# Weight rounding moved ahead of the squares in the paired feed-forward tiles of a two-layer trunk

## The reference, cut to what matters

```python
def squared_relu_mlp(u, w1, w2):
    a = jax.nn.relu(u @ w1)
    return (a * a) @ w2

u = rms_norm(h, ffn_norm_g[i])
h = h + squared_relu_mlp(u, ffn_w1[i], ffn_w2[i])   # w1: 1024 x 4096, w2: 4096 x 1024
```

## Time and profile before

| what | value |
|---|---|
| median of 3 runs | 1159.05 us (1157.74 to 1159.46) |
| profiled execution, its own time | 1157.56 us |
| its span, first to last instruction | 1155.8 us |
| mean granted TensorE clock | 0.994 of full speed |
| TensorE matmul / weight load busy | 1128.4 us / 1050.6 us |
| VectorE busy | 757.6 us (66%) |
| ScalarE busy | 526.5 us (46%) |
| weight loads | 16 DMA engines, 27.2% of their time |

### The profile page before, as it was taken

The page is one execution under the profiler, slowest core; times in us unless marked ns, Lnnn a source line. Parts: engine busy times, 40 slices in busy tenths (PEclk is TensorE's granted clock), DMA queues, the critical chain, the costliest instruction groups (busy, mean ns, idle before and its releaser), DMA issues.

```text
span 1155.8 us, 18677 instructions
## 1 busy us (share of the span) xinstructions
PE 1128.4 (98%) x7817; PEld 1050.6 (91%) x7817; DVE 757.6 (66%) x1063; ACT 526.5 (46%) x826; POOL 2.3 (0%) x30
## 2 busy tenths in 40 slices
PE   6999999999999999999999999999989999999997
PEld 6999999999999999999999888787889899899886
DVE  5898887786785785455353345655786786785443
ACT  6435555454454454333443133543454454454332
POOL 0000000000000000000000000000000000000000
PEclk9999999999999999999899999999999999999999
DMA  6322022233224224222113212132224224224311
GB/s 200 111 74 73 1 74 74 74 107 113 74 93 128 74 81 139 91 93 74 57 54 109 74 43 68 37 109 73 73 74 146 73 74 145 74 86 134 109 37 73
DMA packets 98832, 100.29 MB, mean 87 GB/s; under 512 B 2786, under 2 KB 95644, under 8 KB 98748
## 3 DMA queue, kind: packets, MB, share of 16 engines
q1 hardware_dynamic: 98684, 99.02, 27.2%
q10 hardware_dynamic: 64, 0.07, 0.0%
HBM read 96.99 MB, written 2.10 MB: 86 GB/s over the span
## 4 chain that ended last, share of the span: by engine, by line
PE 81%; DVE 8%; ACT 5%; issue 4%; DMA 1%; SPq 0%; DVEq 0%; ACTq 0%
PE ps L1710 48%; PE ps L1897 20%; PE ps L1963 5%; PE ps L1826 3%; DVE relu L1368 2%; ACT w_hi L487 2%; PE ps L2005 1%; PE ps L2020 1%; DVE w_lo L494 1%; ACT w_hi L525 1%; PE ps L1758 1%; ACT c_hi L877 1%; PE ps L1718 1%; ACT parts L890 1%; DMA raw<-in_cp_w_in_dram 1%
## 5 line engine op out<-in xcount | busy, mean ns | idle before, releaser
L1710 PE MATMUL ps<-u_lo,w_hi 128*128 128x272 f32 (+1 forms) x1120 | 299.6, 323 | 2.2 <-DVE u_lo L1206 2.2
L1710 PE MATMUL ps<-u_hi,w_hi 128*128 128x272 f32 (+1 forms) x1120 | 296.0, 320 | 0.0
L1710 PE MATMUL ps<-u_hi,w_lo 128*128 128x272 f32 (+1 forms) x1120 | 295.6, 320 | 0.0
L494 DVE TENSOR_TENSOR w_lo<-raw,w_hi 128x1024 fp32r<-128x1024 f32 x132 | 161.2, 1224 | 122.5 <-ACT w_hi L487 122.5
L487 ACT ACTIVATE w_hi<-raw 128x1024 fp32r<-128x1024 f32 x132 | 138.4, 1052 | 146.3 <-PE ps L1710 135.4
L1710 PEld LDWEIGHTS ps<-u_lo,w_hi 128*128 128x128 f32 x1120 | 184.4, 189 | 20.2 <-issue 5.2
L1710 PEld LDWEIGHTS ps<-u_hi,w_hi 128*128 128x128 f32 x1120 | 185.2, 190 | 16.1 <-issue 1.2
L1710 PEld LDWEIGHTS ps<-u_hi,w_lo 128*128 128x128 f32 x1120 | 184.1, 188 | 15.4
L1897 PE MATMUL ps<-c_lo,w_hi 128*128 128x264 f32 (+1 forms) x672 | 190.4, 283 | 7.3 <-ACT ps L863 4.8
L1897 PE MATMUL ps<-c_hi,w_lo 128*128 128x264 f32 (+1 forms) x672 | 189.9, 283 | 0.0
L1897 PE MATMUL ps<-c_hi,w_hi 128*128 128x264 f32 (+1 forms) x672 | 189.7, 282 | 0.0
(11 more groups left out here) (239 smaller groups left out, 1550.7 us busy)
## 6 DMA issues: line engine op xcount, KB each, us to landing
raw<-in_ffn_w_dram SPq DMA_DIRECT2D x64, 1024.0 KB, 5.4
raw<-in_gla_w_in_dram SPq DMA_DIRECT2D x12, 1024.0 KB, 5.3
raw<-in_cp_w_in_dram SPq DMA_DIRECT2D x8, 512.0 KB, 5.3
raw<-in_cp_w_out_dram SPq DMA_DIRECT2D x4, 1024.0 KB, 5.0
raw<-in_gla_w_out_dram SPq DMA_DIRECT2D x4, 1024.0 KB, 5.3
xin<-in_x_dram SPq DMA_DIRECT2D x4, 512.0 KB, 5.5
raw<-in_cp_w_in_dram SPq DMA_DIRECT2D x2, 1024.0 KB, 5.0
out_dram<-y_tok SPq DMA_DIRECT2D x4, 512.0 KB, 3.0
```

The source lines that it names most:

```text
L494: dve.tensor_tensor(w_view(w_lo, n), half_view(raw, n), w_view(w_hi, n).bitcast(F32), ALU.subtract).then_inc(w_lo_ready, 1)
L1710: last = mm(ps[:, n % NS, c:c + b - a], l, r[:, a - origin:b - origin], start=(k == 0 and i == 0), stop=(k == count - 1 and i == 2))
```

## The change

In tiles 0 to 3 the weight group goes first: ScalarE rounds it before it waits for the tile's eviction, and VectorE takes the residue right behind the eviction. In tiles 4 to 6 the same is done with the w2 group (in tile 4 behind the sums). In tile 7 the group stays where it was, at the end. No instruction is added or removed and none changes its operands or waits.

```diff
 (ScalarE, paired_ffn)
                     now = parts8[:, j % 2, :, 0:w]
+                    if i < KD // 2:
+                        split_hi(block + i + 4)
+                    elif i < KD - 1:
+                        pair_hi(layer, fb, 0, i - KD // 2)
                     evacuated(act, n)
...
                         act.activation(now[:, E1::E2 - E1, :], src, ACT.Square).then_inc(sq_ready, 1)
-                        if i < KD // 2:
-                            split_hi(block + i + 4)
                         part_hi(E1, T1, 1)
-                        if i >= KD // 2:
-                            pair_hi(layer, fb, 0, i - KD // 2)
...
                         part_hi(T3, T4, 3)
-                        if i < KD // 2:
-                            split_hi(block + i + 4)
-                        else:
+                        if i == KD - 1:
                             pair_hi(layer, fb, 0, i - KD // 2)
 (VectorE, paired_ffn)
                     relu_out(layer, fb, i, tokens)
+                    if i == KD // 2:
+                        pair_sums(layer, fb, 0)
+                    if i < KD // 2:
+                        split_lo(block + i + 4)
+                    elif i < KD - 1:
+                        pair_lo(layer, fb, 0, i - KD // 2)
                     if i % 2 == 0:
-                        if i < KD // 2:
-                            split_lo(block + i + 4)
-                        elif i == KD // 2:
-                            pair_sums(layer, fb, 0)
                         dve.wait_ge(sq_ready, t + 1)
...
                         part_lo(E1, T1, 1)
-                        if i >= KD // 2:
-                            pair_lo(layer, fb, 0, i - KD // 2)
...
                         part_lo(T3, T4, 4)
-                        if i < KD // 2:
-                            split_lo(block + i + 4)
-                        else:
+                        if i == KD - 1:
                             pair_lo(layer, fb, 0, i - KD // 2)
```

## The result

The changed kernel has a median of 1146.77 us (1145.72 to 1149.11, 6 runs) against 1157.61 us (1156.06 to 1159.46, 6 runs) for the kernel before; ratio 0.9901, 95% interval 0.9889 to 0.9914. The direction and the mechanism of the forecast hold.

The account below looks back on a forecast made before the run. TensorE was taken to bound the kernel, with six waits caused by a late VectorE. Gains of 3.0 + 4.5 + 1.4 = 8.9 us, taken as 8.8, gave 1148.8 us profiled and 1150.2 us forecast, range 1148.8 to 1153.2.

Parts of the forecast that it names:

- What bounds the kernel, and where TensorE waits: TensorE, busy 98%; its product matmuls wait six times right behind tile 7, 7.4 us together by the idle column.
- What a wait costs, by starts: Measured between matmul starts, each TensorE wait costs 0.26 us more than the idle column says: 8.9 us in all.
- Why TensorE waits: VectorE is late: in layer 1, block 0, it evicts tile 7 4.5 us late, much of it waiting for ScalarE's `w_hi`.
- New tile lengths, end of the backlog, tile 7's slack: Layer 1, when behind: even tiles 3.56 us, odd 4.90, tile 4 6.01; backlog gone by tile 3 or 4; 0.07 us to spare.
- the sum: Gains of 3.0 us (layer 0, block 0), 4.5 (layer 1, block 0) and 1.4 (layer 1, blocks 1 and 2): 8.9.
- The term for the blocks 0: The first block of each layer gains 3.0 us in layer 0 and 4.5 us in layer 1.
- The range: The measured time would lie between 1148.8 and 1153.2 us.
- Partial: Backlogs vanish, but tile 7's seed still ends late in 4 to 6 blocks; gain 5 to 8 us; chance 0.17.
- no effect: Group rounding still waits for the filled slot, waits come from tile 7; within 2.3 us of 1159.05; chance 0.05.
- The slower one: ScalarE's square queues behind a weight group whose raw load is late; at 7 us late, 1165 us; chance 0.02.

Follow-up runs that it names:

- s0: The changed kernel with only ScalarE's order changed and VectorE in the old order; ratio 0.9902 to the kernel before.
- d1_longer_stall: The changed kernel with three extra copies on ScalarE ahead of tile 7's seed in block 0 of each layer; ratio 0.9958 to the kernel before.
- d2_six_stalls: The changed kernel with three extra copies on ScalarE ahead of tile 7's seed in all six paired blocks; ratio 1.0037 to the kernel before.

## Why the prediction was wrong, point by point

- *What bounds the kernel, and where TensorE waits.* Right. All six waits went, and no other part of the touched stages changed.
- *What a wait costs, by starts.* Right for an execution whose clock stays up: 2.96 + 5.74 = 8.7 us measured against 8.9, where the idle column would have given 7.4.
- *Why TensorE waits.* Right, and narrower than put: s0 shows that ScalarE's late group alone made the backlog.
- *New tile lengths, end of the backlog, tile 7's slack.* Right: 3.47, 4.70 and 6.00 us; on time by tile 3; releases without a wait, with 0.05 us lost in a slower restart.
- **The step that failed is the sum.** It took the six waits at what they cost in one profiled execution and put the clock at nothing. That profile had the granted clock at 1.00 behind every wait. In 5 of 9 blocks 0 with such waits it isn't: the block then takes 1.5 us more, 1.7 us on average over the two blocks 0. The mean over all runs says 1.8 us beyond the waits. The term for the blocks 0 should have been 7.5 + 1.8, with the reservation above on where all of the 1.8 lies.
- *The range.* It took the spread of the runs before, 1.7 us, as noise on either side of the forecast, though its steps were in part the very falls that the change removes. Its low end allowed nothing for that. Another 1.4 us of the miss is the base: the median before was 1159.05 over 3 runs and 1157.61 over 6. With 1157.6 - 8.7 - 1.8 the sum would have been 1147.1.
- *The rivals.* Partial and no effect fell with the waits. The slower one fell by its price as well. It gave the tiles 3.7 us of slack, taking each even tile at its on-time length of 4.0 us. A tile that is behind is shorter, since its group is rounded already. Tiles 0 to 6, when behind, take 3 x 3.47 + 3 x 4.70 + 6.00 = 30.5 us of TensorE's 39.0, so some 8 us can be made good; 3.9 us at tile 1 were gone by tile 6. A load later still was not tried.

## What to carry to other kernels

Where an engine prepares something early for a later stage, put that work ahead of a wait for this stage's own input, if its own inputs are ready by then; the order of the engine that others wait for (here ScalarE) can carry the whole gain. Follow a backlog tile by tile, since chains while behind and chains on time have different lengths. And take the price of a TensorE wait from several executions: one profile shows either the bare wait or the wait with a clock that fell behind it.

## What the runs showed of the hardware

- A TensorE wait of 0.45 us (eight blocks) or 1.3 us (two blocks) was never followed by a fall of the granted clock. Waits of 1.8 to 2.0 us were in 9 of 17 blocks: to 0.50 for about 3 us (in two of them about 7), in which 264-column matmuls started every 0.22 us instead of every 0.12.
- The fall can come with a delay: in d1_longer_stall the first eight matmuls behind the wait still started 0.12 us apart. In d2_six_stalls the clock fell 1.3 and 1.4 us behind the end of the wait.
- Such falls, and the dips at the start and in the value projection, make the run times of this program stand in steps of about 1.6 us rather than spread evenly.
